# Starting a short-convolution projection per request, with early weight loads and results added by DMA

## The reference

```python
x = _layer_norm(ALPHA * x + mix, ln1_g[i], ln1_b[i])
ffn = _grouped_moe(x, router_w, router_b, moe_w_gu[i], moe_w_down[i])   # 16 experts, top 2 of one group
x = _layer_norm(ALPHA * x + ffn, ln2_g[i], ln2_b[i])
```

```python
proj = x @ w_in                      # 1024 x 3072: B, C and h
u = c_gate * hv                      # C * h
conv = conv3(u)                      # depthwise, width 3, over positions of one request
mix = (b_gate * conv) @ w_out        # 1024 x 1024
```

## Time and profile before

| | |
|---|---|
| median of three runs | 996.29 us (995.68 to 996.77) |
| profiled execution | 999.76 us, span 998.0 us |
| busy share of the span | PE 91%, PEld 67%, DVE 50%, ACT 37%, POOL 11% |
| mean granted clock of TensorE | 0.944 of full speed |
| 512 KB loads of expert results, median issue to landing | 7.6 us |

### The profile page before, as it was taken

One profiled execution on the slowest core, in us unless ns is written; L12 is line 12 of the kernel. 1 busy time (PEld: TensorE's weight loads), 2 busy tenths in 40 slices (PEclk: granted clock), 3 DMA queues, 4 the chain that ended last, 5 costly groups with the idle time before them and its releaser, 6 DMA issues. The chain is left out here.

```text
span 998.0 us, 9650 instructions
## 1 busy us (share of the span) xinstructions
PE 905.6 (91%) x3780; PEld 671.4 (67%) x3780; DVE 502.0 (50%) x646; ACT 366.4 (37%) x386; POOL 105.3 (11%) x115
## 2 busy tenths in 40 slices
PE   5999999999789979999999799999899799999920
PEld 2588888877678647676764488888687467676710
DVE  4521121147857546666644913615575465656437
ACT  3222432243311335666642321131313166666520
POOL 2000000040100112121203000000001112121111
PEclk9799999979899989999999899999999989999975
DMA  9023223320307657799936733320256667999362
GB/s 333 31 87 124 85 84 110 101 85 1 126 24 259 226 165 272 283 385 354 347 139 247 252 124 92 120 84 0 84 212 237 222 233 280 399 339 353 135 241 89
DMA packets 80651, 183.75 MB, mean 184 GB/s; under 512 B 10292, under 2 KB 10336, under 8 KB 80608
## 3 DMA queue, kind: packets, MB, share of 16 engines
q1 hardware_dynamic: 69424, 159.53, 44.9%
q0 software_dynamic: 11184, 23.64, 6.8%
HBM read 176.85 MB, written 23.07 MB: 200 GB/s over the span
## 5 line engine op out<-in xcount | busy, mean ns | idle before, releaser
L1098 DVE TENSOR_TENSOR w_lo<-arena,w_hi 128x2048 fp32r<-128x2048 f32 x100 | 229.5, 2297 | 311.1 <-ACT w_hi L876 304.4
L876 ACT ACTIVATE w_hi<-arena 128x2048 fp32r<-128x2048 f32 x100 | 191.0, 1911 | 295.5 <-PE ps L475 292.3
L475 PE MATMUL ps<-w_hi,xt_hi 128*128 128x512 f32 x512 | 204.8, 400 | 5.0 <-DVE xt_lo L1575 3.7
L475 PE MATMUL ps<-w_lo,xt_hi 128*128 128x512 f32 x512 | 201.2, 393 | 0.0
L475 PE MATMUL ps<-w_hi,xt_lo 128*128 128x512 f32 x512 | 200.8, 392 | 0.0
L475 PE MATMUL ps<-xt_hi,w_hi 128*128 128x512 f32 x320 | 126.4, 395 | 3.6 <-DVE w_lo L1098 2.7
L475 PE MATMUL ps<-xt_lo,w_hi 128*128 128x512 f32 x320 | 125.9, 394 | 0.0
L475 PE MATMUL ps<-xt_hi,w_lo 128*128 128x512 f32 x320 | 125.9, 393 | 0.0
L769 PE MATMUL ps<-arena,temp 128*128 128x512 f32 x256 | 115.2, 593 | 2.5 <-ACT temp L990 2.5
L475 PEld LDWEIGHTS ps<-w_hi,xt_hi 128*128 128x128 f32 x512 | 97.4, 190 | 26.2 <-DVE xt_lo L1575 4.1
L475 PEld LDWEIGHTS ps<-w_hi,xt_lo 128*128 128x128 f32 x512 | 97.1, 190 | 20.7
(11 more groups left out here) (200 smaller groups left out, 732.2 us busy)
## 6 DMA issues: line engine op xcount, KB each, us to landing
arena<-in_moe_w_gu SPq DMA_DIRECT2D x64, 1024.0 KB, 11.6
arena<-in_moe_w_down SPq DMA_DIRECT2D x32, 1024.0 KB, 12.7
arena<-in_mlstm_w_in SPq DMA_DIRECT2D x16, 1024.0 KB, 6.3
arena<-in_conv_w_in SPq DMA_DIRECT2D x12, 1024.0 KB, 9.1
arena<-expert_out SPq DMA_DIRECT2D x16, 512.0 KB, 7.6
arena<-in_mlstm_w_out SPq DMA_DIRECT2D x4, 1024.0 KB, 5.0
x_of_experts<-arena SPq DMA_DIRECT2D x8, 512.0 KB, 10.3
arena<-x_of_experts SPq DMA_DIRECT2D x2, 2048.0 KB, 9.5
```

Of the source, the lines that this page charges most:

```text
L475: ins = pe.matmul(out, a, b, start=first and n == 0, stop=last and n == 2)
L876: act.activation(w_hi[:, parity, :], raw(slot), ACT.Copy).then_inc(s_hi, 1)
L1098: dve.tensor_tensor(w_lo[:, parity, :], raw(slot), w_hi[:, parity, :].bitcast(F32), ALU.subtract).then_inc(s_lo, 1)
```

## The change

Four things are changed.

1. SP issues the first six convolution loads before `come_back`; `come_back` loads only the second result of each tile. The taps are loaded during the experts (after the ninth scatter).
2. The first result of each tile is added to the scaled residual by an accumulating DMA that GpSimd issues, so ScalarE scales all four tiles and VectorE has one addition per tile.
3. ScalarE and VectorE split units 0 and 1 ahead of the norm. Units 7 and 13 (u = 7 of each half) are now split within the turn of their half.
4. PE runs the first two units per request: request 0 as soon as its two tiles are split, request 1 after its own; the transposes of tiles 2 and 3 stand between. These matmuls have 256 moving columns. VectorE's order in `expert_norm` follows this, and PE's loop over halves is written out.

```diff
@@ SP, come_back and loads
-                    for k in range(2):
-                        row = k * T + t * P
-                        sp.dma_start(y_back[t][:, k, :], y_dram[layer][row:row + P, :]).then_inc(s_yb[t][k], 16)
+                    row = T + t * P
+                    sp.dma_start(y_back[t], y_dram[layer][row:row + P, :]).then_inc(s_yb[t][1], 16)
...
+            for u in range(RING2):
+                if u % 3 < 2:
+                    sp.wait_ge(s_lo, SPLIT0[0] + 2 * (12 + u // 3) + u % 3 + 1)
+                else:
+                    sp.wait_ge(s_dn, 12 + u // 3 + 1)
+                conv_load(u)
+            come_back(0)
+            for u in range(RING2, MIX2_UNITS):
+                sp.wait_ge(s_lo, SPLIT_CONV + u - RING2 + 1)
+                conv_load(u)
@@ PE
+            def request_features(kh, b, chunks):
+                tok = slice(b * S, (b + 1) * S)
+                for c in chunks:
+                    for k in range(4):
+                        w = slice(k * CG + c * P, k * CG + (c + 1) * P)
+                        x = 4 * kh + k
+                        ins = products(ps[:, c, tok],
+                                       [(w_hi[:, kh, w], xt_hi[:, x, tok]), (w_hi[:, kh, w], xt_lo[:, x, tok]),
+                                        (w_lo[:, kh, w], xt_hi[:, x, tok])],
+                                       kh == 0 and k == 0, kh == 1 and k == 3)
+                    if b == 1 and c == 3:
+                        ins.then_inc(s_hl, 1)
+                    elif b == 1 and kh == 1:
+                        ins.then_inc(s_bank, 1)
...
+            spin(18, 7)
+            conv_T(0)
+            spin(1, 3)
+            conv_T(1)
+            spin(4, 3)
+            pe.wait_ge(s_taps, 1)
+            pe.wait_ge(s_xtl, 20)
+            pe.wait_ge(s_lo, SPLIT_CONV + 1)
+            request_features(0, 0, range(4))
+            conv_T(2)
+            pe.wait_ge(s_lo, SPLIT_CONV + 2)
+            request_features(1, 0, range(2))
+            conv_T(3)
+            request_features(1, 0, range(2, 4))
             pe.wait_ge(s_xtl, 24)
+            request_features(0, 1, range(4))
+            request_features(1, 1, range(4))
+            for half in range(2):
...
+                        if half == 0 and g == 0:
+                            continue
@@ ScalarE
-                for t in (2, 3):
+                for t in range(NT):
                     act.activation(x_back[:, t, :], x_back[:, t, :], ACT.Copy, scale=ALPHA).then_inc(s_ax, 1)
...
+            unit_hi(SPLIT_CONV, 0, raw_count(2, 0), 0)
+            unit_hi(SPLIT_CONV + 1, 1, raw_count(2, 1), 1)
             scale_residual(1)
...
             with act.Fori(0, 2) as half:
-                unit_hi(half * 6 + (SPLIT_CONV + 1), 1, raw_count(2, 1, half), 1)
                 for g in range(3):
                     for kh in range(2):
                         u = 2 * g + kh + 2
-                        if u < 7:
+                        if u < 8:
@@ VectorE, expert_norm
                 scale_and_shift(0)
+                scale_and_shift(1)
                 stat(2)
-                scale_and_shift(1)
+                if call == 1:
+                    half_lo(3, 0)
+                    half_lo(3, 1)
                 stat(3)
@@ VectorE, expert_sum
+                    for k in range(2):
+                        dve.wait_ge(s_yb[t][k], 16 * (call // 2 + 1))
+                    do(dve.tensor_tensor(z[:, t, :], y_back[t], x_back[:, t, :], ALU.add))
@@ VectorE, projection loop
-                unit_lo(half * 6 + (SPLIT_CONV + 1), 1, 1)
                 for g in range(3):
                     for kh in range(2):
-                        if g < 2 or kh == 0:
-                            u = 2 * g + kh + 2
-                            unit_lo(half * 6 + (SPLIT_CONV + u), u % RING2, kh)
+                        u = 2 * g + kh + 2
+                        unit_lo(half * 6 + (SPLIT_CONV + u), u % RING2, kh)
                     for c in range(4):
...
-            unit_lo(SPLIT_CONV + 13, 13 % RING2, 1)
@@ GpSimd
-                for t in (2, 3):
-                    pool.wait_ge(s_ax, 2 * layer + t - 1)
-                    pool.wait_ge(s_yb[t][0], 16 * (layer + 1))
-                    pool.tensor_tensor(x_back[:, t, :], x_back[:, t, :], y_back[t][:, 0, :], ALU.add
-                                       ).then_inc(s_yx, 1)
+                for t in range(NT):
+                    pool.wait_ge(s_ax, NT * layer + t + 1)
+                    pool.dma_start(x_back[:, t, :], y_dram[layer][t * P:(t + 1) * P, :], accum_op=ALU.add
+                                   ).then_inc(s_yb[t][0], 16)
```

More of the change, by code:

```diff
@@ L196, in trunk @@
         conv_rows = temp[0:3 * KC, 2560:2688]
-        y_back = [raw(slot).rearrange("p (k d) -> p k d", k=2) for slot in (6, 7, 8, 11)]
+        y_back = [raw(slot)[:, 0:D] for slot in (6, 7, 8, 11)]
         x_back = words(9 * UNIT, 4096).rearrange("p (t d) -> p t d", t=NT)
@@ L263, in trunk @@
         s_xb = sem("expert_residual_loaded")
-        s_yx = sem("first_result_added")
         s_yb = [[sem(f"result{k}_loaded{t}") for k in range(2)] for t in range(NT)]
@@ L444, in _, with conv_load @@
             late_loads(0)
-            come_back(0)
-            u = 0
             order = [(cw_in, part * D + half * CG) for half in range(2) for part in (1, 2, 0)]
             order += [(cw_out, half * CG) for half in range(2)]
[L450 to L460, removed]
+            def conv_load(u):
+                w, c0 = order[u // 2]
+                load(u % RING2, rows4(w, 4 * (u % 2), c0), 4)
+            for u in range(RING2):
[8 more added lines that the diff above has]
+                conv_load(u)
             expert_loads(1, 0, True)
@@ L839, in _, with conv_T @@
             late_experts(0)
-            def conv_ready(t):
-                if t:
-                    spin(2, 7)
+            def conv_T(t):
                 wait_x(pe, 1, t)
[L845 to L848, removed]
-            pe.wait_ge(s_cwl, 16)
+                if t >= 2:
+                    pe.wait_ge(s_xtl, 16 + 2 * (t - 2) + 2)
+                for half in range(2):
+                    for c in range(4):
+                        f0 = (4 * half + c) * P
+                        ins = pe.transpose(ps[:, 4 + 2 * (t % 2) + half, c * P:(c + 1) * P], z[:, t, f0:f0 + P],
+                                           ident[:, :])
+                    ins.then_inc(s_tr, 1)
@@ new lines, in _ @@
+            pe.wait_ge(s_cwl, 16)
+            pe.transpose(ps[:, 0, 0:3 * KC], conv_rows[:, :], ident[0:3 * KC, 0:3 * KC]).then_inc(s_cwt, 1)
+            spin(18, 7)
[10 more added lines that the diff above has]
+            request_features(1, 0, range(2))
@@ L851, in _ @@
+            conv_T(3)
+            request_features(1, 0, range(2, 4))
             pe.wait_ge(s_xtl, 24)
-            pe.transpose(ps[:, 7, 0:3 * KC], conv_rows[:, :], ident[0:3 * KC, 0:3 * KC]).then_inc(s_cwt, 1)
-            pe.wait_ge(s_taps, 1)
-            with pe.Fori(0, 2) as half:
+            request_features(0, 1, range(4))
+            request_features(1, 1, range(4))
+            for half in range(2):
                 for g in range(3):
                     for kh in range(2):
+                        if half == 0 and g == 0:
+                            continue
@@ L876, in unit_hi, with halves_hi @@
                 act.activation(w_hi[:, parity, :], raw(slot), ACT.Copy).then_inc(s_hi, 1)
-            def halves_hi(stage):
-                for t in range(NT):
+            def halves_hi(stage, tiles=range(NT)):
+                for t in tiles:
                     for half in range(2):
                         act.wait_ge(s_tr, 8 * stage + 2 * t + half + 1)
+                        bank = 4 * half + t if stage < 3 else 4 + 2 * (t % 2) + half
                         act.activation(xt_hi[:, 4 * half:4 * half + 4, t * P:(t + 1) * P],
-                                       ps[:, 4 * half + t, :].rearrange("p (c s) -> p c s", c=4),
+                                       ps[:, bank, :].rearrange("p (c s) -> p c s", c=4),
                                        ACT.Copy).then_inc(s_xth, 1)
@@ L1053, in _ @@
             late_experts(0)
+            unit_hi(SPLIT_CONV, 0, raw_count(2, 0), 0)
+            unit_hi(SPLIT_CONV + 1, 1, raw_count(2, 1), 1)
             scale_residual(1)
[L1055 to L1059, removed]
+            root(1, 0)
+            root(1, 1)
+            halves_hi(3, (0,))
+            root(1, 2)
+            halves_hi(3, (1,))
+            root(1, 3)
+            halves_hi(3, (2, 3))
             with act.Fori(0, 2) as half:
-                unit_hi(half * 6 + (SPLIT_CONV + 1), 1, raw_count(2, 1, half), 1)
                 for g in range(3):
@@ L1074, in _ @@
                 act.activation(xt_hi[:, c, :], g_T[:, c, :], ACT.Copy).then_inc(s_ghx, 1)
-            unit_hi(SPLIT_CONV + 13, 13 % RING2, raw_count(2, 13), 1)
             for n in (14, 15):
@@ L1138, in expert_norm @@
```

(15 more changed lines are left out.)

## The result

The changed kernel takes 1003.5 us (median of 4 runs, 1003.2 to 1006.1) against 996.2 us for the kernel before on the same chip (995.7 to 996.8): ratio 1.0079, interval 1.0061 to 1.0097. That is 7.3 us slower; 2.6 us faster was forecast, and the time lies above the predicted range.

The account below looks back on a forecast made before the run. PE, busy 91% of the span, and VectorE's tail behind it were taken as the bound. Start -13.3, stalls +6.7 and +5.9, tail -1.9 sum to -2.6: 996.3 becomes 993.7 us, range 989.5 to 1002.

Parts of the forecast that it names:

- I take 5.0: Layer 0's norm and the tail: first accumulating transfer lands 5.0 us after issue, as the slowest single 512 KB load.
- When the first sum can start: Layer 0's norm: GpSimd issues at 535.66, the transfer takes 5.0 us, so the first sum starts at 540.7.
- the start's gain: Start of layer 0's projection: first two units end at 582.1 instead of 595.4, gain 13.3 us.
- the tail's: Last norm behind layer 1's experts: VectorE ends at 989.0 instead of 990.85, gain 1.9 us.
- The second stall: Ahead of the output projection: unit 13's split stands before the products, loss 5.9 us, PE gap of 9 us.
- The bounds: Landing of the first accumulating transfer: between 3.6 us, fastest on SP's queue, and 9.1 us, slowest of four back-to-back GpSimd loads.
- The half-rate rival: Both norms: accumulating transfers move at half rate, first landing after 6.3 us, next 3.9 later; 998.7 us, chance 0.28.
- every microsecond of delay counts twice: Landing of the first accumulating transfer: each microsecond later costs in layer 0's norm and again in the tail.
- break-even at 6.3 us: Both norms: the change loses time from a first landing of about 6.3 us.
- uncovered, 5 us: Before the first sum: taps' transpose and copy and the two early splits cost nothing there; uncovered they would cost 5 us.
- The mid-projection stall: Inside the projection: unit 7's split ahead of the products, PE stands 5.0 us plus 1.7 restart, loss 6.7 us.
- paid already: Second stall, ahead of the output projection: PE's restart at the low clock adds nothing to the 5.9 us loss.

Follow-up runs that it names:

- e3_alone: Changed kernel without SyncE's loads of the second results, residual with first result doubled instead, so only its times are of use; 1003.1 us.
- e2_plain: Changed kernel with plain DMAs on GpSimd's queue in place of the accumulating ones, VectorE adding once more per tile; 1013.3 us, one run.
- e6_late: As e5_none, but TensorE starts the projection's products only when all four tiles are transposed and split; 994.6 us, ratio 0.9977.
- e8_splits: As e5_none, but first conv weights loaded behind the experts' results and split behind tile 1's halves; 989.3 us, ratio 0.9915.
- e9_held_only: Changed kernel with both stalls kept, only the first results arranged as in e7_held; 994.5 us, ratio 0.9972.
- e7_held: As e4_two, but the accumulating transfers of tiles 2 and 3 are issued only when tile 1's second result has landed; 979.2 us, ratio 0.9813.
- e5_none: Changed kernel, splits of units 7 and 13 behind the products again, no accumulating transfers: SyncE loads all, GpSimd adds tiles 2 and 3; 983.8 us, ratio 0.9862.
- e4_two: Changed kernel, splits of units 7 and 13 behind the products again, only tiles 2 and 3 accumulating; 983.9 us, ratio 0.9859.

## Why the prediction was wrong

**The step that failed** is "I take 5.0" in *When the first sum can start*. The first accumulating transfer landed after 10.3 and 9.96 us. The step counted twice, as the prediction said it would: 5.3 us of the start's gain (13.3 - 5.3 = 8.0, as measured) and 4.9 of the tail's (-1.9 + 4.9 = +3.0; measured +2.9). Together 10.2; the forecast missed by 9.9 (7.3 + 2.6). The second stall adds 1.0, and the 1.3 that are not placed go the other way.

**Why 5.0 was wrong.** It was the slowest of four plain loads on GpSimd's queue, each with at least one more load behind it, and it was taken because these transfers "move beside SP's result loads". No load of SyncE's was added to it for that. Three runs, each in its tail, take it apart: accumulating without other loads 5.5 us (e3_alone), plain beside SyncE's loads 7.35 (e2_plain), accumulating beside them 9.96. Taking SyncE's loads away is worth 4.4 us, taking the addition away 2.6.

**The bounds failed too.** 9.1 was the slowest of four plain loads issued back to back; no row of before held an operation at half the rate, so no row could be its upper end. What was missing could be had from rows: SyncE's four loads are 2.1 MB, 5.2 us at 405 GB/s, and they are issued 1.7 us earlier (533.99 against 535.66). Put onto the forecast's 5.0, that is an estimate of 8.5 (head start used in full) to 10.2 (not used); put onto the 5.5 of e3_alone, of 9.0 to 10.7. The order in which the engines serve the two was not tried. The tail of the changed kernel speaks against the loads going first: if the longest landing, 9.0 us, is that of the last of SyncE's four, issued at 962.6, it landed at 971.6, where the first landing (964.4) and three times 1.3 us would give an estimate of 968.3.

**The half-rate rival** had the rate right: 210 GB/s against 405. The Trainium skill, Collectives: The Full Stack, section "The bandwidth ceiling: the fold count and why AG ≠ RS ≠ AR", has the reduction of a collective, an addition inside the DMA, half as fast as a copy. These runs agree for an accumulating transfer outside a collective; that a second read is the reason, none of them shows. The rival's price was too low: its 6.3 us to the first landing are the forecast's 5.0 and the 1.3 us of the doubled work, without the four loads that were in flight. Its price for the next tile was too high: it reckoned 3.9 us between the first two sums and a loss of 1.2 in each norm; they stood 3.3 us apart in layer 0, where VectorE waited 0.51 us, and 2.7 in the tail, where it did not wait. Its rule that every microsecond of delay counts twice held; its break-even at 6.3 us was not tried.

**What was right.** The 256-column products stand 0.12 us apart. Starting on the first request is worth 10.8 us by itself (e6_late), the early splits 5.4 (e8_splits; "uncovered, 5 us"). The mid-projection stall was 6.8 for 6.7, with the 5.02 us wait forecast as 5.0. The second stall was 6.9 for 5.9, its wait 9.5 where "one of 9 us" was expected. The wait grew by 5.8 (9.51 against 3.69); the other 1.0 lies in the restart at the low clock, which the prediction called "paid already": from the restart to the unit's end, seen at ScalarE's next conversion that waits for PE, 13.84 us went (707.52 to 721.36), before 12.87 (707.93 to 720.80). With the late first sum mended, the changed kernel takes 994.5 us, near the forecast of 993.7, and its stages lie near the forecast too: the first two units end 13.7 us sooner behind the last expert result than before (forecast 13.3), the two stalls cost 8.1 and 5.8 (6.7 and 5.9), and the tail is 2.5 shorter (1.9). It is not the same code: e9_held_only pays two more additions per layer on VectorE and waits 1.34 us for its first result, so a part of this agreement is luck.

**The clock.** PE idled 8.62 us instead of 3 before the first transposes; they ran at 1.97 us for eight, at a granted clock of 0.50 (the lower of its two levels, 1.2 GHz), much as after 2.41 us in the kernel before (1.94). In e7_held, after 2.42 us, they took 1.09 at the full clock (2.4 GHz). The stretches of these transposes in the changed kernel and in e7_held (columns as above):

```profile
549.70:551.30 1.60, 1.60 (x8) 1.60 (x9) 1.56 (x2) 0.50 (x1) 0.00 (x0) 0.50 1.02 383
```

```profile
544.80:545.80 1.00, 1.00 (x9) 1.00 (x10) 1.00 (x2) 0.30 (x1) 0.00 (x0) 1.00 1.01 233
```

So similar idle times went with either level. The price of a restart varied too: behind the same waits of 5.02 and 9.51 us the two stalls cost 6.8 and 6.9 in the changed kernel, 8.1 and 5.8 in e9_held_only. A restart that one trace shows is no proof for the next one, and the 6.8 for 6.7 of the first stall is in part luck.

## What to carry to other kernels

An addition inside a DMA takes work off an engine, but here it held the DMA engines about twice as long per byte (210 against 405 GB/s): put it behind the transfers that somebody waits for, and use it for the tiles that are needed last (here tiles 2 and 3, worth 4.6 us against e5_none). Price a landing from everything in flight at that moment, not from a row in which little else moved. When a loop is made regular by moving an operation up, look at what it passes on an in-order engine: here two splits ahead of eight small products cost 13.7 us, more than the 8.0 that the new start gained in the changed kernel.

## What the runs showed that was not expected

- Accumulating transfers of 512 KB from DRAM fill the DMA engines at 210 GB/s; plain loads at 405.
- They slow plain loads of other queues: in e4_two VectorE waited 1.95 us for tile 1's load by SyncE, and in e7_held, with the accumulation held back, not at all.
- An accumulating issue holds GpSimd 0.92 us (3.69 for four), a plain one 0.55 (2.18 for four). It was on no critical path here.
